# Weight slots by place in the step, gate and up granules in turn: a mixture-of-experts trunk in split fp32

## The chip, the cores and the metric

The kernel runs on one NeuronCore of a Trainium2 chip. The metric is the device time of one execution in microseconds. Its engines are TensorE (matmuls and transposes), VectorE, ScalarE and GpSimd; SyncE issues nearly all loads. In the profile they are PE, DVE, ACT, POOL and SP.

## The reference

One sequence of 256 tokens with 1024 channels goes through two residual layers. Each has two token mixers side by side (a gated short convolution and a latent attention of 16 heads), merged by sigmoid gates, and then a channel mixer: dense SwiGLU in layer 0, and in layer 1 a SwiGLU of 8 experts, of which each token uses the two with the highest router logits.

```python
def swiglu(t, w_gate, w_up, w_down):
    return (jax.nn.silu(t @ w_gate) * (t @ w_up)) @ w_down
...
for layer in range(DEPTH):                       # DEPTH = 2
    xn = rmsnorm(h, norm_mix[layer])
    proj = xn @ w_in[layer]
    ...
    h = h + (g_a * y_a + g_b * y_b) @ w_mix_out[layer]
    xn = rmsnorm(h, norm_ffn[layer])
    if layer % 2 == 0:
        f = swiglu(xn, dense_w_gate[i], dense_w_up[i], dense_w_down[i])   # width 2816
    else:
        f = moe_swiglu(xn, router_w[i], ...)     # 8 experts, width 1792, top 2
    h = h + f
return rmsnorm(h, norm_final)
```

All inputs and weights are float32.

## The kernel before

Every matmul is done as three. An operand x is split into hi (x rounded to the format fp32r) and lo (x - hi), and `product` adds hi by hi, hi by lo and lo by hi in PSUM (its three matmuls are lines L1171, L1172 and L1173). So each weight goes three ways: SyncE loads it into a raw slot, ScalarE copies it to the hi slot (L519, in the expert stage L659), VectorE subtracts to the lo slot (L785, in the expert stage L990). The engines run programs of their own, in program order, and meet through semaphores that count.

**The dense layer** (`ffn_step`, `silu`, `hidden`, `hidden_hi`, `hidden_lo`) goes through the 2816 hidden channels in 11 blocks of 256. TensorE does the gate and up matmuls of block b in two halves, the transposes of block b - 1's hidden products in between (L1375), then the down matmuls of block b - 1. The last block has no successor: after its gate and up matmuls and the down matmuls of the block before, its own silu (L664), hidden products (L995), transposes, their hi and lo parts (L668, L999) and down matmuls (from L1171) follow one another. Then the result is added to h, and layer 1 begins with a norm (transposes at L1217) and the slabs of `MIX[1]`.

**The router.** After the mixer of layer 1, VectorE scales the tokens (`scale_tokens`, L802), TensorE transposes them, the lo parts are made (`transposed_lo`, L808), and the logits, the top two experts and each token's place in its experts' lists follow in small steps. `split_tokens` (L1089) makes the lo part of the tokens, TensorE gathers the tokens of an expert pair by matmuls with a 0/1 matrix (L1439), and ScalarE and VectorE copy them out (L706, L1129). The lo parts of the first six expert granules are made in between (`expert_lo(0)` to `expert_lo(5)`).

**The expert stage** reads all weights of the 8 experts once. An expert is two steps of 896 hidden channels, so there are 16 steps k. A granule is 128 rows of weights: in step k the places n = 0 to 15 are gate and up granules (128x896, 448 KB; all eight of gate, then all eight of up), the places 16 to 22 are down granules of step k - 1 (128x1024, 512 KB). Step 0 has only places 0 to 15, and a step 16 has only places 16 to 22. That makes 368 granules. Granule i of this list uses raw slot i mod 12 (moved round by 6) and hi and lo slot i mod 6.

The waits of the stage are:

- a load waits until the lo part of the granule before it in its raw slot is made (`RAW_BEFORE`);
- the hi part waits for the load (`e_raw_in`) and until TensorE has used the granule before it in its hi slot (`W_BEFORE`, semaphore `e_used`);
- the lo part waits for the hi part, TensorE for the lo part (`e_lo_made`).

On ScalarE and VectorE the stage is one loop over the granules. At granule i it first converts granule i + 6, then does what belongs to place (k, n): the silu of a step (L723; ScalarE, at place 8, when the gate sums are complete), the hidden products (L1113; VectorE, at place 15), and what `BETWEEN` has put behind a place. `BETWEEN` lists small TensorE jobs with the copies that take their results out of PSUM: "hidden", the transposes of the hidden products of step k - 1 in two parts (L1462, copied at L728 and L1118), at the places 3 and 9 of step k, for step 15 at places 20 and 22 of step 15; "tokens", the gathers of the next pair; "back", the matmuls that bring an expert's output back to its tokens (L1456, L1457, added at L1106). The four sums of a step lie in banks 4 and 5 (gate) and 6 and 7 (up); TensorE waits before place 0 for the silu of the step before and before place 8 for its hidden products.

`second_round` repeats the stage if an expert has more than 128 tokens, which is not the case for these inputs.

## Time and profile before

| what | value |
|---|---|
| median of 3 runs | 1311.43 us (1311.2 to 1311.56) |
| profiled execution | 1311.56 us, span 1309.8 us from first to last instruction |
| PE busy | 1224.0 us (93%) |
| PEld (weight loads of TensorE) busy | 1037.8 us (79%) |
| DVE busy | 917.2 us (70%) |
| ACT busy | 775.6 us (59%) |
| mean granted TensorE clock | 0.975 |
| read from HBM | 294.45 MB, 226 GB/s over the span |

How to read it: the span is the time between the first and the last instruction, the profiled time has 1.8 us around it. The busy time of PE says little about its pace, since matmuls overlap and their ends are modelled. What matters for a change is who waits for whom in the stretch that it touches.

### The profile page before, as it was taken

What the parts mean: (1) busy time and instruction counts of PE and PEld (TensorE: products, weight loads), DVE (VectorE), ACT (ScalarE), POOL (GpSimd) and SP (SyncE); (2) the same over time, 40 slices, a digit from 0 to 9 for tenths busy, and PEclk for the clock granted to TensorE, in tenths of its full rate; (3) what the DMA queues carried; (4) which work ended last, traced back from release to release, by engine and by line L of the source; (5) the groups of instructions that cost most, each with busy time, mean ns of one, the idle gap of its engine ahead of it and who ended that gap; (6) DMA issues with size and microseconds to landing.
All of it is one profiled execution on the core that took longest, in us unless ns stands there. A gap on an engine that the chain in (4) does not pass through costs nothing.

```text
span 1309.8 us, 16219 instructions
## 1 busy us (share of the span) xinstructions
PE 1224.0 (93%) x5901; PEld 1037.8 (79%) x5901; DVE 917.2 (70%) x1160; ACT 775.6 (59%) x1022; POOL 20.7 (2%) x65
## 2 busy tenths in 40 slices
PE   4998999889999979999998969999999999999995
PEld 4887787668888858877786759888888888888884
DVE  5466566665544544576465678899989998999995
ACT  4545466434444324445565338887788878787872
POOL 3000000000000000000000000000000000000000
PEclk9999999999999989999999979999999999999997
DMA  9644622457555334636322638999999999999980
GB/s 322 191 152 161 192 76 88 145 185 279 192 190 179 118 126 144 188 111 203 123 94 87 217 117 299 381 330 342 353 350 334 342 357 340 337 344 354 351 330 34
DMA packets 120382, 296.53 MB, mean 226 GB/s; under 512 B 9028, under 2 KB 33632, under 8 KB 119792
## 3 DMA queue, kind: packets, MB, share of 16 engines
q1 hardware_dynamic: 118720, 288.66, 63.7%
q0 software_dynamic: 1584, 6.88, 1.5%
q8 instruction: 44, 0.72, 0.2%
q14 instruction: 34, 0.28, 0.1%
HBM read 294.45 MB, written 1.05 MB: 226 GB/s over the span
## 4 chain that ended last, share of the span: by engine, by line
PE 84%; DVE 7%; ACT 5%; issue 3%; DMA 1%; POOL 0%; DVEq 0%; SPq 0%; POOLq 0%; ACTq 0%
PE bank L1171 26%; PE bank L1173 25%; PE bank L1172 25%; DVE w_lo L785 2%; ACT w_hi L519 1%; PE bank L1439 1%; DVE proj L889 1%; PE bank L1462 1%; PE bank L1342 1%; PE bank L1322 1%; PE bank L1217 1%; DMA raw<-in_w_in 1%; PE bank L1456 1%; PE bank L1457 1%; PE bank L1314 1%
## 5 line engine op out<-in xcount | busy, mean ns | idle before, releaser
L990 DVE TENSOR_TENSOR w_lo<-raw,w_hi 128x896 fp32r<-128x896 f32 (+1 forms) x368 | 406.4, 1131 | 44.8 <-ACT w_hi L659 36.6
L659 ACT ACTIVATE w_hi<-raw 128x896 fp32r<-128x896 f32 (+1 forms) x368 | 361.7, 988 | 107.3 <-PE bank L1173 105.9
L785 DVE TENSOR_TENSOR w_lo<-raw,w_hi 128x1536 fp32r<-128x1536 f32 (+3 forms) x147 | 246.8, 1685 | 214.6 <-ACT w_hi L519 214.3
L1171 PE MATMUL bank<-w_hi,aT_hi 128*128 128x512 f32 (+2 forms) x848 | 332.6, 392 | 13.8 <-DVE aT_lo L808 7.9
L519 ACT ACTIVATE w_hi<-raw 128x1536 fp32r<-128x1536 f32 (+4 forms) x147 | 209.2, 1427 | 208.3 <-PE bank L1173 201.4
L1173 PE MATMUL bank<-w_hi,aT_lo 128*128 128x512 f32 (+2 forms) x848 | 325.9, 384 | 0.0
L1172 PE MATMUL bank<-w_lo,aT_hi 128*128 128x512 f32 (+2 forms) x848 | 325.0, 383 | 0.0
L1171 PEld LDWEIGHTS bank<-w_hi,aT_hi 128*128 128x128 f32 x848 | 160.8, 190 | 41.7 <-DVE aT_lo L808 9.7
L1173 PEld LDWEIGHTS bank<-w_hi,aT_lo 128*128 128x128 f32 x848 | 160.3, 189 | 27.0
L1172 PEld LDWEIGHTS bank<-w_lo,aT_hi 128*128 128x128 f32 x848 | 160.8, 190 | 24.6
L1171 PE MATMUL bank<-w_hi,bT_hi 128*128 128x448 f32 (+1 forms) x384 | 147.5, 384 | 6.0 <-DVE v L911 4.0
L1173 PE MATMUL bank<-w_hi,bT_lo 128*128 128x448 f32 (+1 forms) x384 | 145.7, 379 | 0.0
L1172 PE MATMUL bank<-w_lo,bT_hi 128*128 128x448 f32 (+1 forms) x384 | 145.5, 379 | 0.0
L1171 PE MATMUL bank<-w_hi,hT_hi_buf 128*128 128x512 f32 x312 | 124.4, 399 | 1.7 <-DVE hT_lo_buf L999 1.7
L1172 PE MATMUL bank<-w_lo,hT_hi_buf 128*128 128x512 f32 x312 | 123.9, 397 | 0.0
L1173 PE MATMUL bank<-w_hi,hT_lo_buf 128*128 128x512 f32 x312 | 123.9, 397 | 0.0
L1171 PEld LDWEIGHTS bank<-w_hi,bT_hi 128*128 128x128 f32 x384 | 73.0, 190 | 17.6 <-issue 4.8
L1172 PEld LDWEIGHTS bank<-w_lo,bT_hi 128*128 128x128 f32 x384 | 73.0, 190 | 10.4
L1173 PEld LDWEIGHTS bank<-w_hi,bT_lo 128*128 128x128 f32 x384 | 72.7, 189 | 10.3
L1171 PEld LDWEIGHTS bank<-w_hi,hT_hi_buf 128*128 128x128 f32 x312 | 59.0, 189 | 15.6 <-DVE hT_lo_buf L999 2.1
L1173 PEld LDWEIGHTS bank<-w_hi,hT_lo_buf 128*128 128x128 f32 x312 | 59.0, 189 | 14.3
L1172 PEld LDWEIGHTS bank<-w_lo,hT_hi_buf 128*128 128x128 f32 x312 | 59.0, 189 | 13.6
(217 smaller groups left out, 995.3 us busy)
## 6 DMA issues: line engine op xcount, KB each, us to landing
raw<-in_moe_w_gate SPq DMA_DIRECT2D x128, 448.0 KB, 4.7
raw<-in_moe_w_up SPq DMA_DIRECT2D x128, 448.0 KB, 4.9
raw<-in_moe_w_down SPq DMA_DIRECT2D x112, 512.0 KB, 5.6
raw<-in_w_in SPq DMA_DIRECT2D x40, 768.0 KB, 4.4
raw<-in_dense_w_gate SPq DMA_DIRECT2D x22, 512.0 KB, 3.9
raw<-in_dense_w_up SPq DMA_DIRECT2D x22, 512.0 KB, 4.8
raw<-in_dense_w_down SPq DMA_DIRECT2D x11, 1024.0 KB, 4.9
raw<-in_w_in SPq DMA_DIRECT2D x20, 512.0 KB, 4.6
```

Of the source, the lines that this page charges most:

```text
L519: act.activation(w_hi[:, j, 0:n], raw[:, b % 2, j, 0:n], ACT.Copy).then_inc(hi_made[j], 1)
L659: act.activation(w_of(hi_slot, i), raw_of(i), ACT.Copy).then_inc(e_hi_made, 1)
L785: dve.tensor_tensor(w_lo[:, j, 0:n], raw[:, b % 2, j, 0:n], w_hi[:, j, 0:n].bitcast(F32), ALU.subtract).then_inc(lo_made[j], 1)
L889: link(*[dve.scalar_tensor_tensor(out=acc[:, c, back:], in0=zT[:, c, 0:S - back], scalar=tap[2 - back][c], in1=acc[:, c, back:], op0=ALU.m ...
L990: dve.tensor_tensor(w_of(lo_slot, i), raw_of(i), w_of(hi_slot, i).bitcast(F32), ALU.subtract).then_inc(e_lo_made, 1)
L1171: pe.matmul(dst, x_hi, b_hi, start=start, stop=False)
L1172: pe.matmul(dst, x_hi, b_lo, start=False, stop=False)
L1173: return pe.matmul(dst, x_lo, b_hi, start=False, stop=stop)
L1217: last = pe.transpose(bank[B_T + n][:, (c % 2) * S + t * P:(c % 2) * S + (t + 1) * P], xs[:, t, c * P:(c + 1) * P], ident[:, :])
L1314: last = pe.transpose(bank[B_QK][0:QK, m * S + t * P:m * S + (t + 1) * P], src[:, t, n * QK:(n + 1) * QK], ident[:, :])
L1322: last = pe.matmul(bank[B_S][:, t * P:(2 * t + 1) * P], qkT[0:QK, t * P:(t + 1) * P], qkT[0:QK, S:S + (t + 1) * P], start=True, stop=True)
L1342: last = pe.matmul(bank[B_O][:, t * VD:(t + 1) * VD], pT[:, m * P:(m + 1) * P], v[:, kt, (n - 3) * VD:(n - 2) * VD], start=start, stop=stop)
```

## The change

Five things change, all in the order and the places of the work; what is computed stays.

1. Slots go by place: granule (k, n) uses raw slot n mod 12 (moved round by 6) and hi and lo slot n mod 6. `slot_history` looks up which granule had the slot before.
2. Gate and up granules alternate: place n is chunk n // 2 of gate (n even) or up (n odd). So the gate sums are complete at place 14, the silu moves to place 15, and TensorE waits before place 0 for the hidden products of the step before.
3. The last hidden transposes (step 15) and their copies move from places 20 and 22 of step 15 to places 14 and 15 of step 16, which have no granules: directly before (16, 16).
4. At the end of the dense layer, the conversions of the first two slabs of layer 1 and the last silu and hidden products come before the conversion of the last down slab.
5. Around the router, the lo parts of the granules 2 and 3 are made behind `transposed_lo`, those of 4 and 5 behind `split_tokens`.

```diff
 def slot_history(slots):
-    return [i - slots if i >= slots else None for i in range(len(GRANULES))]
-RAW_BEFORE, W_BEFORE = slot_history(RAW_SLOTS), slot_history(W_SLOTS)
+    last, before, turn = {}, [], []
+    for i, (_, _, n) in enumerate(GRANULES):
+        prev = last.get(n % slots)
+        before.append(prev)
+        turn.append(0 if prev is None else turn[prev] + 1)
+        last[n % slots] = i
+    return before, turn
+RAW_BEFORE, RAW_TURN = slot_history(RAW_SLOTS)
+W_BEFORE, _ = slot_history(W_SLOTS)
...
-BETWEEN[STEPS - 1, 20], BETWEEN[STEPS - 1, 22] = ("hidden", STEPS - 1, 0), ("hidden", STEPS - 1, 1)
+BETWEEN[STEPS, 14], BETWEEN[STEPS, 15] = ("hidden", STEPS - 1, 0), ("hidden", STEPS - 1, 1)
...
         def raw_of(i):
-            return raw_slot[:, (i + RAW_SLOTS // 2) % RAW_SLOTS, 0:granule_width(GRANULES[i][2])]
+            return raw_slot[:, (GRANULES[i][2] + RAW_SLOTS // 2) % RAW_SLOTS, 0:granule_width(GRANULES[i][2])]
         def w_of(slots, i):
-            return slots[:, i % W_SLOTS, 0:granule_width(GRANULES[i][2])]
+            return slots[:, GRANULES[i][2] % W_SLOTS, 0:granule_width(GRANULES[i][2])]
...
-                                w, c, col = (moe_w_gate, moe_w_up)[n // KC][0], n % KC, k % 2 * HALF
+                                w, c, col = (moe_w_gate, moe_w_up)[n % 2][0], n // 2, k % 2 * HALF
...
             def expert_hi(i):
-                act.wait_ge(e_raw_in[i % RAW_SLOTS], 16 * (i // RAW_SLOTS + 1))
+                _, _, n = GRANULES[i]
+                act.wait_ge(e_raw_in[n % RAW_SLOTS], 16 * (RAW_TURN[i] + 1))
...
             ffn_step(F + DENSE - 1, DENSE - 1, F, False)
+            hi(MIX[1], 0, LAT_SIZES[0], MIX[1])
+            silu(F + DENSE - 1, DENSE - 1)
+            hi(MIX[1], 1, LAT_SIZES[1], MIX[1])
             hi(F + DENSE - 1, 2, SLOT, F, True)
-            silu(F + DENSE - 1, DENSE - 1)
-            hi(MIX[1], 0, LAT_SIZES[0], MIX[1])
             hidden_hi(DENSE - 1)
-            hi(MIX[1], 1, LAT_SIZES[1], MIX[1])
...
             def expert_silu(r, k):
-                act.wait_ge(e_used, SEQ[r, k, KC - 1] + 1)
-                if r or k:
-                    act.wait_ge(e_hid_made, 2 * (STEPS * r + k))
+                act.wait_ge(e_used, SEQ[r, k, GU_N - 1] + 1)
...
                     _, k, n = GRANULES[i]
+                    if (k, n) == (STEPS, GU_N):
+                        between(STEPS, 14)
+                        between(STEPS, 15)
                     if i + W_SLOTS < PER_ROUND * (r + 1):
                         expert_hi(i + W_SLOTS)
-                    if n == KC:
+                    if n == GU_N - 1:
                         expert_silu(r, k)
...
             ffn_step(F + DENSE - 1, DENSE - 1, False)
+            lo(MIX[1], 0, LAT_SIZES[0])
             hidden(DENSE - 1)
+            lo(MIX[1], 1, LAT_SIZES[1])
             lo(F + DENSE - 1, 2, SLOT)
             hidden_lo(DENSE - 1)
-            lo(MIX[1], 0, LAT_SIZES[0])
-            lo(MIX[1], 1, LAT_SIZES[1])
...
             square_tile(3)
-            expert_lo(2)
             scale_tokens(3)
-            expert_lo(3)
             transposed_lo(7, aT_lo, aT_hi)
-            for i in range(4, W_SLOTS):
-                expert_lo(i)
+            expert_lo(2)
+            expert_lo(3)
...
                 if r == 0:
                     split_tokens()
+                    for i in range(4, W_SLOTS):
+                        expert_lo(i)
...
             def gate_up_granule(r, k, n):
-                i, c, p, x = SEQ[r, k, n], n % KC, k // 4, k // 2 % 2
-                if k % 4 == 0 and n in range(0, KC, 2):
+                i, c, p, x = SEQ[r, k, n], n // 2, k // 4, k // 2 % 2
+                if k % 4 == 0 and n % 4 == 0:
                     pe.wait_ge(x_lo_in, 4 * (EXPERTS // 2 * r + p) + c // 2 + 1)
                 if n == 0:
                     if k % 4 == 0:
                         pe.wait_ge(x_hi_in, 4 * (EXPERTS // 2 * r + p) + 4)
                     if r or k:
-                        pe.wait_ge(e_silu_made, 2 * (STEPS * r + k))
-                if n == KC and (r or k):
-                    pe.wait_ge(e_hid_made, 2 * (STEPS * r + k))
+                        pe.wait_ge(e_hid_made, 2 * (STEPS * r + k))
                 pe.wait_ge(e_lo_made, i + 1)
```

The products of a granule go to `bank[(B_GATE, B_UP)[n % 2][u]]` instead of `[n // KC]`, and waits on the raw slots use n in place of i in the same way in `expert_loads`; the first hi parts wait for `used[n // 2]`.

## Rows read from the trace of the kernel before

**Rows 1.** Windows: length, busy us (instructions) of PE, PEld, DVE, ACT, POOL; clock, DMA share, GB/s.

```profile
820.00:850.00 30.00, 30.00 (x151) 26.67 (x150) 26.60 (x27) 24.19 (x29) 0.00 (x0) 1.00 1.01 382
...
1150.00:1250.00 100.00, 100.00 (x480) 87.48 (x479) 91.72 (x95) 78.92 (x90) 0.00 (x0) 1.00 0.98 351
```

**Rows 2.** Timeline of ScalarE, 795 to 812: start, us, operation, count, idle before.

```profile
797.77 1.28 ACT L723 ACT_TABLE_LOAD   x1
799.06 0.98 ACT L723 ACTIVATE sg_buf<-bank 128x448 f32<-128x448 f32 x2
799.92 5.16 ACT L659 ACTIVATE w_hi<-raw 128x896 fp32r<-128x896 f32 x6
805.31 0.95 ACT L659 ACTIVATE w_hi<-raw 128x896 fp32r<-128x896 f32 x1 [0.23 <-PE bank L1173]
806.52 0.95 ACT L659 ACTIVATE w_hi<-raw 128x896 fp32r<-128x896 f32 x1 [0.26 <-PE bank L1173]
```

**Rows 3.** Waits of the DMA queue, 785 to 1292: us in total, times, longest.

```profile
SPq L432 <- DVE w_lo L990: 370.8, 350, 16.6
```

**Rows 4.** Timeline of ScalarE near the end of the expert stage.

```profile
1276.78 1.06 ACT L659 ACTIVATE w_hi<-raw 128x1024 fp32r<-128x1024 f32 x1 [0.34 <-PE bank L1173]
1278.17 1.06 ACT L659 ACTIVATE w_hi<-raw 128x1024 fp32r<-128x1024 f32 x1 [0.34 <-PE bank L1173]
...
1280.54 0.58 ACT L728 ACTIVATE hT_hi_buf<-bank 128x512 fp32r<-128x512 f32 x1
```

**Rows 5.** Timeline of TensorE: four restarts after idle time.

```profile
477.29 1.11 PE L1375 MATMUL bank<-ident,hid_buf 128*128 128x128 f32 x4 [3.12 <-DVE hid_buf L995]
480.09 0.79 PE L1171 MATMUL bank<-w_hi,hT_hi_buf 128*128 128x512 f32 x1 [1.69 <-DVE hT_lo_buf L999]
...
493.20 3.65 PE L1217 MATMUL bank<-ident,xs 128*128 128x128 f32 x16 [5.69 <-DVE xs L802]
...
764.16 3.68 PE L1217 MATMUL bank<-ident,xs 128*128 128x128 f32 x16 [5.38 <-DVE xs L802]
```

**Rows 6.** Timeline of ScalarE and VectorE, 474 to 478: the last down slab.

```profile
474.27 1.91 ACT L519 ACTIVATE w_hi<-raw 128x2048 fp32r<-128x2048 f32 x1 [10.53 <-PE bank L1173]
...
477.15 2.29 DVE L785 TENSOR_TENSOR w_lo<-raw,w_hi 128x2048 fp32r<-128x2048 f32 x1
```

**Rows 7.** Timeline of VectorE around the router, 760 to 785.

```profile
762.82 2.48 DVE L802 SCALAR_TENSOR_TENSOR xs<-h,small,gain 128x1024 f32<-128x1024 f32 x2 [0.94 <-POOL small L473]
765.22 1.09 DVE L990 TENSOR_TENSOR w_lo<-raw,w_hi 128x896 fp32r<-128x896 f32 x1
767.23 2.48 DVE L808 TENSOR_TENSOR aT_lo<-bank,aT_hi 128x512 fp32r<-128x512 f32 x4 [0.92 <-ACT aT_hi L534]
...
783.86 1.29 DVE L1129 CAST aT_lo<-bank 128x512 fp32r<-128x512 f32 x2 [2.46 <-PE bank L1439]
```

**Rows 8.** Timeline of VectorE, 795 to 812: the hidden products of step 0.

```profile
807.93 1.15 DVE L1113 TENSOR_TENSOR hid_buf<-sg_buf,bank 128x448 f32<-128x448 f32 x2
```

**Rows 9.** Timeline of TensorE: the first matmul of (1, 0).

```profile
805.05 0.36 PE L1171 MATMUL bank<-w_hi,aT_hi 128*128 128x448 f32 x1
```

**Rows 10.** The expert loads issued from 728 to 795.

```profile
DMA to landing us min/median/max: 3.2/4.0/6.0
```

**Rows 11.** Timeline of VectorE near the end of the expert stage.

```profile
1276.11 5.79 DVE L990 TENSOR_TENSOR w_lo<-raw,w_hi 128x1024 fp32r<-128x1024 f32 x5
1281.81 0.68 DVE L1118 TENSOR_TENSOR hT_lo_buf<-bank,hT_hi_buf 128x512 fp32r<-128x512 f32 x1
```

**Rows 12.** Timeline of TensorE: behind (15, 22), and the start of (16, 16).

```profile
1282.54 0.49 PE L1462 MATMUL bank<-ident,hid_buf 128*128 128x128 f32 x3
1282.79 0.48 PE L1171 MATMUL bank<-w_hi,hT_hi_buf 128*128 128x512 f32 x1
```

**Rows 13.** Windows, columns as in rows 1: two stretches at half clock.

```profile
490.36:497.18 6.82, 3.65 (x16) 3.28 (x16) 4.37 (x5) 2.02 (x5) 0.81 (x2) 0.50 0.27 77
763.42:770.25 6.83, 5.86 (x27) 4.66 (x28) 5.91 (x8) 3.65 (x6) 0.62 (x1) 0.50 0.56 196
```

More of the change, by code:

```diff
@@ L421, in expert_loads @@
                             if RAW_BEFORE[i] is None:
-                                s = (i + RAW_SLOTS // 2) % RAW_SLOTS
+                                s = (n + RAW_SLOTS // 2) % RAW_SLOTS
                                 sp.wait_ge(lo_made[s % 6 // 2], MIX[1] + (BLK_MIX, BLK_MIX + 1)[s < RAW_SLOTS // 2] + 1)
@@ L431, in expert_loads @@
                                 src = moe_w_down[0][(k - 1) // 2, row:row + P, :]
-                            sp.dma_start(raw_of(i), src).then_inc(e_raw_in[i % RAW_SLOTS], 16)
+                            sp.dma_start(raw_of(i), src).then_inc(e_raw_in[n % RAW_SLOTS], 16)
                     expert_loads(0)
@@ L653, in expert_hi @@
             def expert_hi(i):
-                act.wait_ge(e_raw_in[i % RAW_SLOTS], 16 * (i // RAW_SLOTS + 1))
+                _, _, n = GRANULES[i]
+                act.wait_ge(e_raw_in[n % RAW_SLOTS], 16 * (RAW_TURN[i] + 1))
                 if W_BEFORE[i] is None:
-                    act.wait_ge(used[i // 2], MIX[1] + BLK_MIX + 2)
+                    act.wait_ge(used[n // 2], MIX[1] + BLK_MIX + 2)
                 else:
@@ L1150, in experts @@
                     _, k, n = GRANULES[i]
+                    if (k, n) == (STEPS, GU_N):
+                        between(STEPS, 14)
+                        between(STEPS, 15)
                     if i + W_SLOTS < PER_ROUND * (r + 1):
@@ L1478, in gate_up_granule @@
                     part = slice(u * HN, (u + 1) * HN)
-                    last = product(bank[(B_GATE, B_UP)[n // KC][u]][:, 0:HN], tile(x_hiT[p % 2], c, x), tile(x_loT[p % 2], c, x),
+                    last = product(bank[(B_GATE, B_UP)[n % 2][u]][:, 0:HN], tile(x_hiT[p % 2], c, x), tile(x_loT[p % 2], c, x),
                                    w_of(hi_slot, i)[:, part], w_of(lo_slot, i)[:, part], c == 0, c == KC - 1)
```

## The prediction, made before the change was run

> **What bounds the kernel now.** Read the busy time by stretches first [rows 1]. In the expert stage, which runs from 785 to 1293 us, TensorE is busy for 100 of 100 us at the full clock, and VectorE is next with 91.7 of 100. The question there is not what is busy but which engine is waited for. ScalarE's timeline says it [rows 2]: its splits of a weight granule begin with a bracket that names TensorE (0.23 to 0.26 us idle, then release). ScalarE waits for a granule to be used, while TensorE's 100 of 100 leaves no room for a wait of its own. The DMA queue's own waits [rows 3] say the same of the loads: 350 of them wait for VectorE to free a raw slot, none is late for anybody. So the stage's time is the sum of TensorE's own work, and anything that leaves TensorE without input is added in full to the end. A change to slots or order can only win in front of the stage or in its tail.
>
> I write a granule as (k, n): step k, place n. From [rows 2], TensorE takes 1.21 us for a gate or up granule (two releases, 805.31 and 806.52) and from [rows 4] 1.40 us for a down granule (1276.78 to 1278.17). ScalarE and VectorE do everything in program order, and their loops convert granule i + 6 before they do what belongs to granule i. This order is what the argument hangs on.
>
> **Part 1, end of the dense layer: a gain of 0.9 us.** Today ScalarE converts the last down slab (1.91 us from 474.27) [rows 6] before the silu, so the hidden products come late: TensorE sits idle 3.12 us until they are there (477.29), transposes, and is idle 1.69 us more until 480.09 [rows 5]. The new order puts the silu ahead of that conversion. Its inputs are there several us earlier, since the gate/up matmuls precede the down matmuls that end near 474.2. The transposes then follow those directly. What is late next is the slab itself: its hi part still ends at 474.27 + 1.91 = 476.18, its lo part (2.29 us, today from 477.15 because VectorE was at the hidden products) starts at 476.2 and ends at 478.5, hT_lo adds about 0.6, and TensorE starts at 479.2 instead of 480.1: 0.9 us. The two conversions of the next layer's first slabs, moved forward, fall into ScalarE's and VectorE's idle time ahead of 474. Nothing after it has slack against TensorE's path, so 0.9 is kept. Bounds: 0 (the clock eats it) to 1.5.
>
> **Part 2, in front of the router: nothing.** The lo parts of (0,2) and (0,3) leave the places beside scale_tokens. (0,3) takes 1.09 us, and VectorE is idle 0.94 and 0.92 us at these two places even so, waiting for GpSimd and ScalarE [rows 7]: scaling starts no sooner. They take the place that (0,4) and (0,5) had, and these go behind the token split, in front of a 2.46 us wait (783.86). Two of them need 2.1 us. Cost 0; without that cover, 2.1. TensorE wants (0,4) only near 790.
>
> **Part 3, slots by place.** With slot n mod 6, places 0 to 4 of a step reuse the slots of places 18 to 22, so they may be converted five granules ahead, not six. Six ahead, the slack between lo part and use is 5 x 1.21 = 6.1 us less 0.1 release, 0.95 for the hi part and 1.09 for the lo part, near 3.9; one down granule less leaves 2.5. Positive, with VectorE free for 8% of the time to catch up: 0 for the 14 ordinary boundaries. The raw slots are 11 instead of 12 deep there, also 0. Moving the silu from place 8 to place 15 costs nothing in an ordinary step: seven down granules (9.8 us) lie between it and the next place 0. Two boundaries are not ordinary.
>
> *The first, (0,15) to (1,0).* Step 0 has no down granules. So slots for (1,0) to (1,3) were last used by (0,12) to (0,15), and TensorE now waits at (1,0) for the hidden products of step 0. ScalarE's order is hi of (1,0), ..., (1,5), then the silu. The release by (0,15) is the one at 805.31 [rows 2]; those by (0,12), (0,13), (0,14) lie 1.21 apart before it, at 801.7, 802.9, 804.1. Hence hi (1,3) runs 805.3 to 806.3, hi (1,4) and (1,5) follow 0.84 apart (six take 5.16 in rows 2) and end at 807.95. Then the table for the silu, 1.29 us to the activation behind it (797.77 to 799.06, [rows 2]), then two silus in 0.98, the first done near 809.8. VectorE's two products take 1.15 [rows 8]: 810.95. TensorE starts (1,0) at 811.0, today at 805.05 [rows 9]: **6.0 us**.
>
> The table load is here what the row shows, 1.28 us. The Trainium skill (ScalarE: Activation LUTs, "What ACT_TABLE_LOAD costs") has the same 1283 ns and adds a drain of some 1.38 us to each switch; no gap of that size stands behind the load in this row, and by the page this stall would be 7.4 us.
>
> Do the loads keep up? The raw slot of (1,0) is now free only when the lo part of (0,12) is made. Its release is nine granules of 1.21 before 805.31, 794.4; with 0.95 and 1.09 it is 796.5. A copy lands in 3.2 us at best, 4.0 in the median [rows 10]; the engines move 382 GB/s [rows 1], a 459 KB granule in 1.2 us. So (1,0) lands at about 800, before its 801.7; (1,3), freed by the lo part of (0,15) near 800.1, at 804.5; (1,5) at 806.9, just when ScalarE comes to it. Hidden by the stall above, with nothing to spare; bound from above 1.5 us.
>
> *The last, (15,22) to (16,16).* Place 16 takes the slot of place 22, used one granule ago. ScalarE comes to hi (16,16) early and stands there until TensorE has finished (15,22). Behind it stand five more hi parts and, after these, the two copies of the last hidden transposes, which the down granules of step 16 need; VectorE has the same order. TensorE ends (15,22) today just after the transposes' start at 1282.54 [rows 12]; four transposes (0.33 us by three in 0.25) no longer lie before it, so the release is at about 1282.5. Hi (16,16): to 1283.5. VectorE's six lo parts: five take 5.79 [rows 11], six 6.95, so to 1290.5. ScalarE's six (1.06 each, rows 4) and its 0.58 copy end at about 1289.6, earlier. Then hT_lo, 0.68 less overlap: 1291.1. TensorE starts (16,16) at 1291.15, today 1282.79: **8.4 us**. The lo parts of the six granules are then ready, the second half of hT_lo comes 0.6 later and isn't late.
>
> **Part 4, the clock.** After idle times of 5.69 and 5.38 us [rows 5] TensorE ran at a granted 0.50, the 1.2 GHz level, in the stretches of [rows 13], with 3.65 and 5.86 us of work in them. Half of such work is lost time: 1.8 and 2.9, mean 2.35 for each stall, and both stalls (6.0 and 8.4) are longer than these idle times. Twice 2.35 is 4.7. Bounds per stall: 0 and 3.4 (all of a 6.8 us stretch busy).
>
> **Sum**, on the profiled execution: 1311.56 (span 1309.8, with 1.8 around it) - 0.9 + 6.0 + 8.4 + 4.7 = 1329.8. The median of the runs is 1311.43, 0.1 lower: 1329.6.
>
> **The rivals.**
> - *The loads become late.* With the queue held back until 796.5, its lead shrinks from twelve granules to four at (1,0). For: the queue already waits for slots all along [rows 3], and 351 to 382 GB/s are nearly what the stage takes. Against: TensorE's stall gives the queue 6 us to catch up. If (1,5) and the granules behind it come late all the same, 1.5 to 6 us more: 1331 to 1336.
> - *The clock stays up.* TensorE has run without a pause for long before both stalls. Against: both of [rows 13]. Without 4.7: 1325.
> - *Five slots are too few at ordinary boundaries.* It decides where VectorE falls more than 2.5 us behind; at 91.7% busy it gathers such a lag only if several extras meet. If the 14 boundaries lose 1 us each: 1344.
> - *Not slower:* both stalls are covered and only the front counts. The place is the dense end: if TensorE's idle there gets short enough that the clock doesn't fall, the half-speed work until 497.2 is saved too (3.65 us of transposes and perhaps 4 of down matmuls, half of it lost now, about 4): 1306.7 to 1310.7. It decides only where the two stalls together cost under 5 us, against 14.4 worked out; for this ScalarE would have to do its later work past an instruction that waits, which nothing in rows 2 shows.
>
> **How the numbers follow.** My forecast 0.80, late loads 0.07, clock up 0.06, boundaries 0.04, not slower 0.03. The time is the forecast's. Own bounds: front 0 to 1.5, stall one 5.5 to 7.5, stall two 7.8 to 9, clock 3.6 to 6.8 together give 1327.0 to 1334.9 at the corners. The range 1323.5 to 1335 takes in the clock case and most of the late loads. About 0.2% (2.6 us) is what a measurement of this kernel can tell from no change: faster 0.02, same 0.02, slower 0.96.
>
> **What would show it.** In the changed profile: TensorE idle about 6 us in front of the first matmul of (1,0), released by VectorE's hidden product, with ScalarE's table load just ahead; a second idle of about 8.4 us starting some 38 us before the end, released by hT_lo, behind six conversions in a row on ScalarE and VectorE; a granted clock of 0.50 behind both; no TensorE wait between. At the dense end the 3.12 us idle gone and one of about 4 us in its place. If TensorE waits for lo parts in ordinary steps, the slack of part 3 was wrong; if ScalarE waits for a DMA at (1,4) or (1,5), the loads were; if (16,16) starts on time, I misread the order in which ScalarE reaches the copies.

## The result: 1.8% slower, and where the time goes

The changed kernel takes 1334.9 us in the median (1332.6 to 1337.6), against 1311.5 before: ratio 1.0176, 95% interval 1.0155 to 1.0198. The forecast was 1329.6, from 1323.5 to 1335: right in direction and in the two stalls, wrong in front of the expert stage, and 5.3 us too low in all. The measured time lies 0.1 us inside the upper end of the range.

The first lines of the page after. TensorE has the same 5901 matmuls. Against the page of before, its clock is lower in slice 15 (7 in place of 8: the dense end), in slice 22 (8 in place of 9, in front of the expert stage too), in slice 25 (8 in place of 9: the first stall) and in the last (6 in place of 7).

```profile
span 1331.9 us, 16189 instructions
PE 1231.1 (92%) x5901; PEld 1043.2 (78%) x5901; DVE 919.5 (69%) x1160; ACT 772.3 (58%) x1022; POOL 20.8 (2%) x65
PEclk9999999999999979999998988999999999999996
```

TensorE's timeline after, at places that divide the kernel (its matmuls are L1183 to L1185 now): the restarts at the end of the dense layer, the starts of (0,0), (1,0), (2,0) and (16,16).

```profile
476.95 0.79 PE L1183 MATMUL bank<-w_hi,hT_hi_buf 128*128 128x512 f32 x1 [4.55 <-DVE hT_lo_buf L1008]
...
786.30 0.36 PE L1183 MATMUL bank<-w_hi,aT_hi 128*128 128x448 f32 x1
...
813.90 0.74 PE L1183 MATMUL bank<-w_hi,aT_hi 128*128 128x448 f32 x1 [7.18 <-DVE hid_buf L1120]
...
846.55 0.37 PE L1183 MATMUL bank<-w_hi,aT_hi 128*128 128x448 f32 x1
...
1302.49 0.79 PE L1183 MATMUL bank<-w_hi,hT_hi_buf 128*128 128x512 f32 x1 [7.98 <-DVE hT_lo_buf L1125]
```

Before, these four starts lie at 785.15, 805.05 [rows 9], 835.08 and 1282.79 [rows 12], and the last instruction ends at 1309.84. The differences give the whole account:

| stretch | before | after | more | forecast |
|---|---|---|---|---|
| start to (0,0) | 785.15 | 786.30 | 1.15 | -0.9 |
| (0,0) to (1,0) | 19.90 | 27.60 | 7.70 | 6.0 |
| (1,0) to (2,0) | 30.03 | 32.65 | 2.62 | 2.35 |
| (2,0) to (16,16) | 447.71 | 455.94 | 8.23 | 8.4 |
| (16,16) to the end | 27.05 | 29.44 | 2.39 | 2.35 |
| sum | 1309.84 | 1331.93 | 22.09 | 18.2 |

This is one execution of each kernel; the medians differ by 1.3 us more, 23.4. And the first row is not what the change costs in front. The last matmul before the idle time at the end of the dense layer starts at 473.77 before and at 471.56 after, though the change touches nothing ahead of it: this execution lacks a stretch at half clock near 101 us and has a shorter one near 229 us, worth 2.2 us together. From that matmul to (0,0) it is 311.38 us before and 314.74 after, 3.4 more, where 0.9 less was forecast. The section on the front takes that up.

Both stalls stand where they were forecast. ScalarE's timeline at the first, to be read against [rows 2]:

```profile
803.10 0.95 ACT L667 ACTIVATE w_hi<-raw 128x896 fp32r<-128x896 f32 x1 [2.76 <-PE bank L1185]
804.34 0.95 ACT L667 ACTIVATE w_hi<-raw 128x896 fp32r<-128x896 f32 x1 [0.29 <-PE bank L1185]
805.58 0.96 ACT L667 ACTIVATE w_hi<-raw 128x896 fp32r<-128x896 f32 x1 [0.28 <-PE bank L1185]
806.87 0.95 ACT L667 ACTIVATE w_hi<-raw 128x896 fp32r<-128x896 f32 x1 [0.34 <-DMA raw<-in_moe_w_up]
808.75 0.95 ACT L667 ACTIVATE w_hi<-raw 128x896 fp32r<-128x896 f32 x1 [0.93 <-DMA raw<-in_moe_w_gate]
809.86 0.95 ACT L667 ACTIVATE w_hi<-raw 128x896 fp32r<-128x896 f32 x1 [0.16 <-DMA raw<-in_moe_w_up]
810.83 1.28 ACT L729 ACT_TABLE_LOAD   x1
812.12 0.98 ACT L729 ACTIVATE sg_buf<-bank 128x448 f32<-128x448 f32 x2
```

These are the hi parts of (1,0) to (1,5), then the table and the silus, with TensorE idle behind them. The first three wait for TensorE's use of (0,12) to (0,14), as worked out; the last three wait for their loads. At the end of the stage, ScalarE and VectorE do what [rows 4, 11] let one expect, six conversions in a row ahead of the copies:

```profile
1293.85 5.79 ACT L667 ACTIVATE w_hi<-raw 128x1024 fp32r<-128x1024 f32 x6 [6.92 <-PE bank L1185]
1299.54 0.95 ACT L734 ACTIVATE hT_hi_buf<-bank 128x512 fp32r<-128x512 f32 x2
```

```profile
1294.93 6.90 DVE L999 TENSOR_TENSOR w_lo<-raw,w_hi 128x1024 fp32r<-128x1024 f32 x6 [6.09 <-ACT w_hi L667]
1301.75 1.15 DVE L1125 TENSOR_TENSOR hT_lo_buf<-bank,hT_hi_buf 128x512 fp32r<-128x512 f32 x2
```

ScalarE stands for 6.92 us at hi (16,16), held by the granule just before it. And the clock, in windows as in [rows 13]: behind the dense end and behind each stall.

```profile
488.04:498.28 10.24, 7.12 (x26) 6.64 (x27) 5.90 (x7) 2.06 (x4) 0.45 (x1) 0.50 0.17 51
808.89:819.13 10.24, 5.22 (x14) 4.66 (x15) 4.49 (x6) 5.26 (x7) 0.00 (x0) 0.50 1.03 411
1297.00:1307.24 10.24, 4.75 (x11) 3.78 (x12) 6.54 (x8) 4.55 (x6) 0.00 (x0) 0.50 0.00 0
```

TensorE works 5.22 and 4.75 us at half clock behind the stalls. Half of that, 2.6 and 2.4, is what the table shows there.

### The profile page after: what moved, and what is told of

Read it like the earlier page. It is cut to its first block, busy times and chain, and to the rows that moved or that the text cites. A ratio compares the mean times of both kernels' runs of the same rounds, so it can differ in the third digit from the quotient of the medians.

```text
span 1331.9 us, 16189 instructions
## 1 busy us (share of the span) xinstructions
PE 1231.1 (92%) x5901; PEld 1043.2 (78%) x5901; DVE 919.5 (69%) x1160; ACT 772.3 (58%) x1022; POOL 20.8 (2%) x65
## 4 chain that ended last, share of the span: by engine, by line
PE 83%; DVE 7%; ACT 5%; issue 3%; DMA 1%; POOL 0%; SPq 0%; DVEq 0%; POOLq 0%; ACTq 0%
PE bank L1183 25%; PE bank L1185 25%; PE bank L1184 25%; ACT w_hi L526 2%; DVE w_lo L794 2%; PE bank L1451 1%; DVE proj L898 1%; PE bank L1354 1%; PE bank L1334 1%; PE bank L1474 1%; PE bank L1229 1%; DMA raw<-in_w_in 1%; PE bank L1468 1%; PE bank L1469 1%; DVE w_lo L999 1%
## 5 line engine op out<-in xcount | busy, mean ns | idle before, releaser
L667 ACT ACTIVATE w_hi<-raw 128x896 fp32r<-128x896 f32 (+1 forms) x368 | 357.2, 985 | 130.6 <-PE bank L1185 128.0
L1183 PE MATMUL bank<-w_hi,aT_hi 128*128 128x512 f32 (+2 forms) x848 | 334.7, 395 | 20.9 <-DVE aT_lo L817 7.8
L1185 PE MATMUL bank<-w_hi,aT_lo 128*128 128x512 f32 (+2 forms) x848 | 327.4, 386 | 0.0
L1183 PEld LDWEIGHTS bank<-w_hi,aT_hi 128*128 128x128 f32 x848 | 162.0, 191 | 49.5 <-DVE aT_lo L817 9.7
L1185 PEld LDWEIGHTS bank<-w_hi,aT_lo 128*128 128x128 f32 x848 | 161.5, 190 | 27.4
L1183 PE MATMUL bank<-w_hi,bT_hi 128*128 128x448 f32 (+1 forms) x384 | 147.4, 384 | 6.0 <-DVE v L920 4.0
L1185 PE MATMUL bank<-w_hi,bT_lo 128*128 128x448 f32 (+1 forms) x384 | 145.7, 379 | 0.0
L1183 PE MATMUL bank<-w_hi,hT_hi_buf 128*128 128x512 f32 x312 | 125.4, 402 | 12.5 <-DVE hT_lo_buf L1125 8.0
L1185 PE MATMUL bank<-w_hi,hT_lo_buf 128*128 128x512 f32 x312 | 124.8, 400 | 0.0
L1183 PEld LDWEIGHTS bank<-w_hi,bT_hi 128*128 128x128 f32 x384 | 73.0, 190 | 17.6 <-issue 4.8
L1185 PEld LDWEIGHTS bank<-w_hi,bT_lo 128*128 128x128 f32 x384 | 72.8, 190 | 10.2
L1183 PEld LDWEIGHTS bank<-w_hi,hT_hi_buf 128*128 128x128 f32 x312 | 59.7, 191 | 26.7 <-DVE hT_lo_buf L1125 8.2
L1185 PEld LDWEIGHTS bank<-w_hi,hT_lo_buf 128*128 128x128 f32 x312 | 59.6, 191 | 14.5
```

The costliest lines, as they stand in the source:

```text
L667: act.activation(w_of(hi_slot, i), raw_of(i), ACT.Copy).then_inc(e_hi_made, 1)
L1183: pe.matmul(dst, x_hi, b_hi, start=start, stop=False)
L1185: return pe.matmul(dst, x_lo, b_hi, start=False, stop=stop)
```

## The experiments

Ratios are to the kernel before, on the same chip. Idle times are the brackets in each kernel's TensorE timeline.

### What makes the stalls

**All slots by count again**, the rest as changed.

```diff
-RAW_BEFORE, RAW_TURN = slot_history(RAW_SLOTS)
-W_BEFORE, _ = slot_history(W_SLOTS)
+RAW_BEFORE = [i - RAW_SLOTS if i >= RAW_SLOTS else None for i in range(len(GRANULES))]
+RAW_TURN = [i // RAW_SLOTS for i in range(len(GRANULES))]
+W_BEFORE = [i - W_SLOTS if i >= W_SLOTS else None for i in range(len(GRANULES))]
...
 # raw_of, w_of and e_raw_in use i in place of the place n
```

> The changed kernel with all slots given by count again (12 raw, 6 hi and lo), everything else as changed. Theory A (both stalls are made by the slots by place, behind which ScalarE's and VectorE's later work stands in order; the order of gate and up adds its part at the first boundary): before (1,0) TensorE idles about 4.2 us (hi of (1,5) after the release by (0,15), 1.3 table load, 1.0 silus, 0.7 product), before (16,16) about 2.6 us; 1321 to 1324. Rival B (the alternation of gate and up with the silu at place 15 makes the first stall, the moved transposes the second, and the slots do nothing): idles of 7.2 and 8.0 us as in the changed kernel, 1333 to 1336.

Measured: 1324.9 us, ratio 1.0104 (1.0085 to 1.0123). TensorE's two restarts:

```profile
810.05 0.74 PE L1184 MATMUL bank<-w_hi,aT_hi 128*128 128x448 f32 x1 [4.14 <-DVE hid_buf L1121]
...
1292.89 0.50 PE L1184 MATMUL bank<-w_hi,hT_hi_buf 128*128 128x512 f32 x1 [2.30 <-DVE hT_lo_buf L1126]
```

4.14 and 2.30 us, where 4.2 and 2.6 were expected (the time is 0.9 us above the 1321 to 1324). So the slots by place make 3.0 and 5.7 us of the two stalls. By what is left of the change, the rest should belong to the silu at place 15, whose products TensorE needs with no down granules in between, and to the moved transposes; no run takes either of them back alone with the slots by count, so this is argued and not shown.

**The raw slots alone by count.**

```diff
-RAW_BEFORE, RAW_TURN = slot_history(RAW_SLOTS)
+RAW_BEFORE = [i - RAW_SLOTS if i >= RAW_SLOTS else None for i in range(len(GRANULES))]
+RAW_TURN = [i // RAW_SLOTS for i in range(len(GRANULES))]
...
 # raw_of and e_raw_in use i in place of the place n
```

> The changed kernel with the raw slots alone given by count again. Theory A (the first stall is 1.3 us longer than forecast because the loads of (1,3) to (1,5) land late): ScalarE no longer waits for a landing there, the idle before (1,0) is 5.9 us instead of 7.2, the one before (16,16) stays near 8.0; 1.3 us faster than the changed kernel in the stage. Rival B (the loads were only just in time and something else is long): idle stays 7.2.

Measured: 1332.8 us, ratio 1.0161 (1.0140 to 1.0181). The interval overlaps that of the changed kernel, so the time alone says nothing; the rows do. ScalarE:

```profile
807.47 0.96 ACT L668 ACTIVATE w_hi<-raw 128x896 fp32r<-128x896 f32 x1 [0.26 <-PE bank L1186]
808.68 2.63 ACT L668 ACTIVATE w_hi<-raw 128x896 fp32r<-128x896 f32 x3 [0.26 <-PE bank L1186]
811.33 1.28 ACT L730 ACT_TABLE_LOAD   x1
```

TensorE:

```profile
814.40 0.74 PE L1184 MATMUL bank<-w_hi,aT_hi 128*128 128x448 f32 x1 [5.82 <-DVE hid_buf L1121]
...
1302.13 0.79 PE L1184 MATMUL bank<-w_hi,hT_hi_buf 128*128 128x512 f32 x1 [7.98 <-DVE hT_lo_buf L1126]
```

The hi parts of (1,3), (1,4) and (1,5) run in one piece of 2.63 us, nobody waits for a load, and the idle time is 5.82 us in place of 7.18; the second stays at 7.98. The late loads cost 1.4 us. From (0,0) to (1,0) this kernel takes 25.88 us, 5.98 more than before: the 6.0 that were forecast without late loads. Theory A holds.

**The hi and lo slots alone by count.**

```diff
-W_BEFORE, _ = slot_history(W_SLOTS)
+W_BEFORE = [i - W_SLOTS if i >= W_SLOTS else None for i in range(len(GRANULES))]
...
-            return slots[:, GRANULES[i][2] % W_SLOTS, 0:granule_width(GRANULES[i][2])]
+            return slots[:, i % W_SLOTS, 0:granule_width(GRANULES[i][2])]
```

> The changed kernel with the hi and lo slots alone given by count again, raw slots by place. Theory A: the idle before (16,16) shrinks from 8.0 to 2.6 us, since hi (16,16) no longer waits for (15,22); the one before (1,0) shrinks little, to about 7, since hi of (1,3) to (1,5) still waits for late loads; 1326 to 1329. Rival B (the first stall too is the hi slots' doing alone): idle before (1,0) 4.2 us and a time like that with all slots by count, 1321 to 1324.

Measured: 1329.2 us, ratio 1.0138 (1.0119 to 1.0157).

```profile
813.03 0.74 PE L1183 MATMUL bank<-w_hi,aT_hi 128*128 128x448 f32 x1 [6.87 <-DVE hid_buf L1120]
...
1296.15 0.50 PE L1183 MATMUL bank<-w_hi,hT_hi_buf 128*128 128x512 f32 x1 [2.30 <-DVE hT_lo_buf L1125]
```

6.87 and 2.30 us: theory A (the time is 0.2 us above its range). What the slots add at the second stall, 5.7 us, is the hi and lo slots' alone. At the first, two things hold ScalarE one behind the other: the late loads, which end last, and the hi slots, about 1 us sooner. Freeing the raw slots alone wins 1.4 us, freeing the hi and lo slots alone 0.3, and both together 3.0.

**The last transposes put back.**

```diff
-BETWEEN[STEPS, 14], BETWEEN[STEPS, 15] = ("hidden", STEPS - 1, 0), ("hidden", STEPS - 1, 1)
+BETWEEN[STEPS - 1, 20], BETWEEN[STEPS - 1, 22] = ("hidden", STEPS - 1, 0), ("hidden", STEPS - 1, 1)
```

> The changed kernel with the last hidden transposes and their copies put back to places 20 and 22 of step 15, slots by place kept. Theory A (the second stall is the slot of (16,16), not the moved transposes): ScalarE comes to the first copy after hi of (16,16) to (16,19), four conversions instead of six, so TensorE still idles before (16,16), 6.0 us in place of 8.0; 1332 to 1334. Rival B (the move of the transposes made the stall): it starts on time, 1323 to 1326.

Measured: 1331.9 us, ratio 1.0152 (1.0125 to 1.0179); TensorE idles 6.14 us before (16,16). ScalarE's timeline shows the four conversions in front of the first copy:

```profile
1296.97 3.90 ACT L667 ACTIVATE w_hi<-raw 128x1024 fp32r<-128x1024 f32 x4 [7.34 <-PE bank L1185]
1300.77 0.57 ACT L734 ACTIVATE hT_hi_buf<-bank 128x512 fp32r<-128x512 f32 x1
```

TensorE's transposes are early again, and it helps little, since their copies still stand behind hi (16,16). Theory A.

**The ready work first.** ScalarE's and VectorE's order alone is altered, at the two places.

```diff
-                    if (k, n) == (STEPS, GU_N):
+                    if (k, n) == (STEPS - 1, GU_N + 1):
                         between(STEPS, 14)
                         between(STEPS, 15)
+                    if (k, n) == (0, 13):
+                        expert_silu(r, k)
                     if i + W_SLOTS < PER_ROUND * (r + 1):
                         expert_hi(i + W_SLOTS)
-                    if n == GU_N - 1:
+                    if n == GU_N - 1 and k:
                         expert_silu(r, k)
```

VectorE's loop has the same edit with `expert_lo` and `expert_hidden`.

> The changed kernel with ScalarE's and VectorE's order alone altered at the two places: the silu and the hidden products of step 0 come before the conversion of (1,3), and the copies of the last hidden transposes before the conversion of (16,16). Slots, loads and TensorE's program stay. Theory A (what makes the stalls is that ready work stands behind conversions that wait): before (1,0) TensorE idles 3.2 us in place of 7.2 (release 0.1, table 1.3, silus and products 1.7), before (16,16) about 3.2 in place of 8.0 (copy 0.6, hT_lo 0.7, then hi 1.1 and lo 1.2 of (16,16), overlapped in part); 1324 to 1327. Rival B (the slots themselves, one granule old, make the stalls): idles within 1 us of the old ones, 1332 or more.

Measured: 1324.0 us, ratio 1.0097 (1.0070 to 1.0125), just under the 1324 to 1327 of theory A. TensorE:

```profile
810.71 0.74 PE L1187 MATMUL bank<-w_hi,aT_hi 128*128 128x448 f32 x1 [2.94 <-DVE hid_buf L1122]
...
1293.34 0.47 PE L1187 MATMUL bank<-w_hi,hT_hi_buf 128*128 128x512 f32 x1 [3.03 <-DVE w_lo L1001]
```

With the slots by place untouched, both stalls shrink to 3 us. Ready work behind a conversion that waits makes 4.2 us of the first and 5.0 of the second; the young slot is what makes the conversion wait. In the second, TensorE now waits for the lo part of (16,16) itself (L1001): these 3.03 us are what the young slot costs with the order mended. The kernel is still 0.97% slower than before, by these two idle times and by the dense end (below).

### What the clock takes

**The stalls filled.**

```diff
+                    if k == 1:
+                        for _ in range(80):
+                            pe.transpose(bank[0][:, 0:P], ident[:, :], ident[:, :])
                     if r or k:
                         pe.wait_ge(e_hid_made, 2 * (STEPS * r + k))
...
+                if k == STEPS and c == 0:
+                    for _ in range(88):
+                        pe.transpose(bank[4][:, 0:P], ident[:, :], ident[:, :])
```

> The changed kernel with 80 extra transposes of a constant on TensorE in front of its wait before (1,0) and 88 in front of (16,16), whose results nobody reads: they fill the two stalls without making them shorter. Theory A (the half clock behind the stalls costs 2.6 and 2.2 us, and TensorE's being busy in them avoids it): no half-clock stretch behind the two places, 4.8 us faster than the changed kernel, near 1330. Rival B (transposes don't count for the clock, or the clock isn't what costs): 1334 to 1335, half clock as before.

Measured: 1331.8 us, ratio 1.0155 (1.0128 to 1.0182), not the 1330 expected. The windows at and behind the two places:

```profile
806.00:816.00 10.00, 10.00 (x86) 9.84 (x85) 6.92 (x8) 6.48 (x8) 0.00 (x0) 1.00 0.99 374
816.00:826.00 10.00, 10.00 (x55) 9.28 (x54) 6.82 (x11) 6.65 (x8) 0.00 (x0) 1.00 1.03 409
1292.00:1303.00 11.00, 11.00 (x96) 10.68 (x95) 7.97 (x8) 6.65 (x8) 0.00 (x0) 1.00 0.01 4
1303.00:1313.00 10.00, 10.00 (x49) 8.23 (x48) 1.22 (x1) 1.06 (x1) 0.00 (x0) 1.00 0.01 2
```

The clock stays at 1.00, at full rate, through both stalls and behind them. From (1,0) to (2,0) this kernel takes 30.1 us, after 32.65, before 30.03. But the filling was too long:

```profile
807.61 8.89 PE L1486 MATMUL bank<-ident 128*128 128x128 f32 x80
...
1294.14 9.77 PE L1502 MATMUL bank<-ident 128*128 128x128 f32 x88
```

8.89 and 9.77 us of it stand in stalls of 7.2 and 8.0, and delay (1,0) and (16,16) by 1.3 and 1.4 us. Behind the first place 2.5 us are won back. Behind the second it is 2.2: from (16,16) to the next idle time, in front of the "back" matmuls, this kernel takes 12.16 us, after 14.31, before 12.15. 4.7 us won back less 2.7 lost is 2.0, and the ratios differ by 0.0021, 2.8 us; their intervals overlap, so the windows show it and not the times. Theory A holds as to the clock.

### The front

**Both reorderings in front of the expert stage**, on the kernel before (the edits of points 4 and 5 of the change).

> The kernel before with the two reorderings in front of the expert stage alone (end of the dense layer, lo parts around the router). Theory A (the step as forecast holds, and the 1.15 us that the changed kernel's profile is late at the first expert granule are granted-clock stretches that fall differently from execution to execution): at the dense end the 3.12 us idle is gone and one of 4.5 us stands there, the last down matmuls start 0.9 us earlier against the matmuls before them; the time is 1311.5 less 0.9, 1309.5 to 1311.5. Theory B (the reordering itself brings more half-speed stretches behind the dense end, 0.9 gained and about 3 lost): 1312.5 to 1314.

Measured: 1313.7 us, ratio 1.0017 (1.0005 to 1.0030). Theory B: slower, not faster.

**One at a time**: the dense end alone (point 4), and the router alone (point 5).

> The kernel before with the reordering at the end of the dense layer alone. Both reorderings together measured 0.17% slower than before, where 0.07% faster was forecast. Theory A (the longer unbroken idle of 4.55 us and what follows it let the granted clock stay at half for longer behind the dense end; every profile with this reordering shows 10.2 us at half clock there, the one of before 6.8): this part alone is 1.5 to 3 us slower than before, 1313 to 1314. Theory B (the router's part costs it): this part is 0.9 faster, 1310.3.

> The kernel before with the moved lo parts around the router alone. Theory A (hidden at both places, as forecast): 1311.2, within 0.1%. Theory B (the two lo parts behind the token split hold up the copies of the gathered tokens): 1 to 2.5 us slower, 1312.5 to 1313.5.

Measured: the dense end 1314.8 us, ratio 1.0023 (1.0009 to 1.0037), 0.8 us above theory A's range, with before at 1313.0 in these runs; the router 1313.1 us, ratio 1.0004 (0.9990 to 1.0018). So the router's part is the zero that was forecast, and the dense end costs 0.2%. The window behind the dense end in the kernel with the dense end alone, and then in that with the router alone:

```profile
492.10:502.30 10.20, 7.19 (x26) 6.68 (x27) 5.81 (x7) 2.06 (x4) 0.34 (x1) 0.50 0.17 51
```

```profile
491.80:498.60 6.80, 3.65 (x16) 3.28 (x16) 4.24 (x5) 2.00 (x5) 0.91 (x2) 0.50 0.27 77
```

The first has 7.19 us of TensorE's work at half clock, the second 3.65, as before had [rows 13]. The 3.5 us more cost 1.8, less than half of what this kernel loses. The largest part of the rest stands further on. Windows of the kernel with the dense end alone, and then of that with the router alone at the same matmuls:

```profile
580.84:584.25 3.41, 3.41 (x10) 2.63 (x9) 1.46 (x2) 0.00 (x0) 0.00 (x0) 0.50 0.77 231
707.14:713.96 6.82, 5.06 (x15) 4.00 (x15) 4.00 (x7) 0.00 (x0) 1.46 (x4) 0.50 0.71 208
```

```profile
577.50:582.50 5.00, 4.21 (x18) 3.44 (x19) 3.54 (x3) 0.32 (x1) 0.00 (x0) 1.00 0.50 142
706.90:710.30 3.40, 3.40 (x10) 2.62 (x9) 1.92 (x3) 0.00 (x0) 0.00 (x0) 0.50 0.50 191
```

TensorE's program is the same in before and in the kernel with the dense end alone, so their profiles can be laid side by side matmul by matmul, counted from the last matmul before the idle time at the dense end. The last dense down starts 0.94 us sooner, as forecast. At 505 us the kernel is 1.15 us late, behind the stretch at 581 us 2.75, behind that at 707 us 3.4, and so it comes to (0,0). All nine kernels with this reordering and no filling there lose 2.9 to 3.8 us on this way.

**The dense end with its idle times filled.**

```diff
 # the kernel before with point 4 of the change, and
             def transpose_normed(N):
+                for _ in range({2: 38}.get(N, 0)):
+                    pe.transpose(bank[7][:, 0:P], ident[:, :], ident[:, :])
...
             hidden_transposes(DENSE - 1)
+            for _ in range(37):
+                pe.transpose(bank[7][:, 0:P], ident[:, :], ident[:, :])
             down(F + DENSE - 1, DENSE - 1, False, True)
```

> The kernel before with the reordering at the end of the dense layer, and extra transposes of a constant on TensorE, results unread, in its two idle times there (37 in the one of 4.55 us, 38 in the one of 5.7). Theory A (the reordering gains 0.9 us and the clock behind it takes 2 to 3 away): without the half-clock stretches at 478 and 492 the gain shows, and what before too lost there (half of 3.4 and 4.0 us) comes back: 0.9 + 3.5 = 4.4 us faster than before, near 1307.5. Rival B (the reordering costs through something else than the clock): 1311 or more.

Measured: 1308.6 us, ratio 0.9973 (0.9957 to 0.9988), 0.27% faster than before, and in the window

```profile
470.00:505.00 35.00, 31.65 (x193) 28.20 (x192) 17.91 (x19) 10.99 (x17) 0.91 (x2) 1.00 0.30 98
```

the clock is 1.00 throughout (before: 0.80 in the same window). With the half-clock stretches gone the loss is gone too: the clock is what the reordering cost. The gain is 3.5 us of the 4.4 expected by the ratio, 2.7 by the medians. Most of it is what before too loses there, and before wasn't run with these two places alone filled. That the reordering's own 0.9 us is in it can be read from the profiles: from the last matmul before the dense end's idle time to 560 us this kernel takes 3.3 us less than before, and before with its own idle times there filled (next experiment) takes 2.4 us less.

**All long idle times filled**, without and with the reordering.

```diff
 # the kernel before, and
+                for _ in range({1: 38, 2: 38, 3: 45}.get(N, 0)):        # transpose_normed
+            for _ in range(24):                                         # before hidden_transposes(DENSE - 1)
+            for _ in range(11):                                         # before the last dense down
+            for _ in range(18):                                         # before the wait for chosen_made
+                for _ in range(13):                                     # before the gathers
```

Each is a loop of the same transpose into bank 7, which nobody reads. With the reordering, 37 stand before the last dense down in place of the 24 and 11.

> The kernel before, order unchanged, with extra transposes of a constant on TensorE in its long idle times before the expert stage (38, 24, 11, 38, 45, 18 and 13 of them, each a little shorter than the idle time it fills). Theory A: the half-clock stretches at 289, 477, 490, 763 and 777 us go; half of the work in them, 1.7 + 1.7 + 2.0 + 2.9 + about 2.2, comes back: 8 to 11 us faster than before, 1301 to 1304. Rival B (the clock's loss is only shifted, or the extra work delays what it precedes): less than 3 us.

> The same as the kernel with the filled idle times, with the reordering at the end of the dense layer too. Theory A (the clock out of the way, the reordering is worth its 0.9 us): 0.9 us faster than that kernel, 1300 to 1303. Rival B (the reordering costs by itself): 1.5 to 2 us slower than that kernel.

Measured: without the reordering 1305.0 us, ratio 0.9952 (0.9936 to 0.9969); with it 1306.0 us, 0.9955 (0.9939 to 0.9971). The first is 6.3 us faster than before, under the 8 to 11 expected, and the fastest version of this study. In its profile 0.6 us come back at 289 us, 2.4 at the dense end and 2.9 around the router, where 1.7, 3.7 and 5.1 were expected; why so little, no run tests. In its page no slice of the clock row but the last is under 0.9:

```profile
PEclk9999999999999999999999999999999999999998
```

The two don't differ by what can be measured, so neither theory about the second is borne out. Their TensorE timelines show why the 0.9 us can vanish even so. Without the reordering, then with it, at the next idle time that isn't filled:

```profile
573.38 0.50 PE L1171 MATMUL bank<-w_hi,aT_hi 128*128 128x512 f32 x1 [2.04 <-DVE w_lo L785]
```

```profile
571.81 0.80 PE L1171 MATMUL bank<-w_hi,aT_hi 128*128 128x512 f32 x1 [2.08 <-DVE w_lo L785]
```

With it TensorE is there 1.6 us sooner (0.9 of it from the reordering, 0.6 from ahead of the dense end), after an idle time of the same length; but there the clock falls, and in the other it doesn't. The windows with it and without it:

```profile
571.80:575.20 3.40, 3.39 (x8) 2.72 (x9) 2.76 (x2) 0.00 (x0) 0.00 (x0) 0.50 0.55 168
```

```profile
571.80:575.20 3.40, 1.82 (x8) 1.50 (x9) 3.40 (x3) 1.12 (x2) 0.00 (x0) 1.00 0.22 48
```

The lead is lost in this stretch. It is the same place as 581 us in the kernel with the dense end alone. The idle time in front of it is 2.04 to 2.08 us in all 14 profiles. A stretch of 3.4 us at half clock follows it in this one and in the nine with the reordering unfilled; none follows in before, with the router alone, in before filled and with the dense end filled. What decides it, no run shows.

## Why the prediction came out as it did

- **The number.** The medians differ by 23.4 us, and 18.2 were forecast. In the terms of the sum: the front cost about 3.4 us where 0.9 were to be gained, the loads 1.4 where nothing was put in, the clock 0.3 more, the last stall 0.2 less (24.0 in all, read from single profiles). That the time is still in the range is luck: the front lies outside its own bounds (0 to 1.5 gained), and the room for it was meant for late loads.
- **What bounds the kernel** held. TensorE's idle time shows in full in the end; from (2,0) to (16,16) the only thing that changed is the last stall.
- **Part 1** failed. The mechanism was right: after the matmuls before it, the last dense down starts 0.9 us sooner; the 3.12 us idle is gone and one of 4.55 us stands there (forecast: about 4). What failed is "Nothing after it has slack against TensorE's path, so 0.9 is kept" with its bounds of 0 to 1.5. I took the path behind as rigid and counted the clock only behind the new stalls. In its place the runs show a loss of 0.23% for this part alone (0.09 to 0.37%). In the profiles it is 3.4 us: 0.9 gained, and 4.3 lost in half-clock stretches that are longer or new behind the dense end, near 581 and near 707 us. It is gone when the idle times are filled. The first row of the table shows only 2.0 us of this miss of 4.3, since the changed kernel's profile came to the dense end 2.2 us early, for a reason that lies ahead of all that the change touches.
- **Part 2** held: 1.0004 (0.9990 to 1.0018).
- **Part 3, ordinary boundaries**, held: no TensorE wait and no time between (2,0) and (15,22).
- **Part 3, first boundary**: the mechanism held, the size was 1.7 us short. The term was the loads, "hidden by the stall above, with nothing to spare; bound from above 1.5 us"; it measured 1.4 (7.18 against 5.82 us idle). I let each load land about 1.2 us behind the last, and my 804.5 for (1,3) had no working (800.1 and a median of 4.0 give 804.1). But once (1,3) is issued at 801.49 the queue finds the slots behind it free and issues the next at 801.88, 802.35 and 802.83. With the engines' share at 0.99 in this stretch, I read the longer landing times as loads that share the engines with those behind them; no run tests that. Landing times of the three loads before and of the six from (1,3) on:

```profile
DMA to landing us min/median/max: 3.4/4.3/4.4
```

```profile
DMA to landing us min/median/max: 5.4/7.8/9.2
```

  The other 0.3 us is a slightly slower pace of TensorE in step 0 of this one profile (15 granules in 19.0 us instead of 18.7), which none of the six variants of it has. Its cause stays open.
- **The table load** was again followed by the silu 1.29 us after its start. The Trainium skill (ScalarE: Activation LUTs, "What ACT_TABLE_LOAD costs") would have made the stall 7.4 us with its drain, close to the 7.18 measured; but the kernel with the raw slots by count has the same load and idles 5.82. The agreement was an accident.
- **Part 3, last boundary**: 8.23 measured, 8.4 forecast.
- **Part 4**: 2.6 and 2.4 measured, 2.35 forecast for each, and shown by the filled stalls. (The range took 3.6 to 6.8 for both, while the bounds of this part are 0 to 6.8; the low end of the sum was set too high.)
- **The rivals**: late loads came in part, inside the forecast's own bound. The clock didn't stay up, five slots sufficed, and the dense end did the opposite of what the "not slower" case wanted.

## What to carry to other kernels

Where an engine converts some items ahead and does its other work in the same program, ask at each wrap of the slots what stands behind a conversion that must wait for a young slot: that work is late by the whole run of conversions. Here TensorE idled 8.0 us for 0.6 us of copying, and 3.0 with the copying first. Slots by place are as good as slots by count only while all periods are alike; look at the first and the last one, where there are none of the usual items in between. And a gain of one microsecond on TensorE's path isn't kept by itself: what the clock does behind it, here up to 230 us further on, can weigh more. To find such a loss, lay the two profiles side by side at matmuls that both have.

## What the runs showed of the hardware

- Transposes of a constant keep the clock up: 8.89 us of nothing else, at 1.00 and with 1.00 for the 9 us behind it. One takes about 0.11 us at the full clock, and 187 of them in seven idle times made the kernel 0.48% faster (0.31 to 0.64%).
- The same idle time doesn't always cost the same: of 14 idle times of 2.04 to 2.08 us before the same matmul, ten were followed by 3.4 us at half clock and four by none.
- Much of the scatter between executions goes with the clock. Of 25 executions of the kernel before, ten took 1308.0 to 1310.2 us at a mean granted clock of 0.978 or 0.979, and fifteen 1311.1 to 1317.1 us at 0.972 to 0.975.
- Nine loads of 448 KB, issued every 0.4 to 1.2 us, landed after 3.4 to 4.4 us while few were under way and after 5.4 to 9.2 us when issued in a burst.
